# Extra TensorE products of constants placed in five waits of a hybrid backbone kernel

## The reference

```
a    = modulate(rmsnorm(h), shift, scale)
even: y = concat(ssd(...), mlstm(...)) @ w_out     # layer 0, after group norms and gates
odd:  y = concat(window_attention, dense_attention) @ w_out   # layer 1, latent tokens only
h    = h + g1 * y
t    = modulate(rmsnorm(h), sh2, sc2)
route: group = top-1 of softmax(t @ w_group); experts = top-2 of 4 inside the group
moe  = sum over the two experts of gate * (silu(t @ w_gate) * (t @ w_up)) @ w_down
h    = h + g2 * moe
out  = rmsnorm(h_latent)
```

## Time and profile before

| | us |
|---|---|
| median of 3 runs | 1970.26 |
| lowest, highest | 1960.47, 1976.62 |
| the profiled execution, its own time | 1980.49 |
| its span, first to last instruction | 1978.8 |
| mean granted TensorE clock | 0.907 |
| PE busy | 1652.3 (84%) |
| PE weight loads busy | 1006.2 (51%) |
| DVE busy | 848.1 (43%) |
| ACT busy | 520.5 (26%) |
| POOL busy | 273.1 (14%) |

### The profile page before, as it was taken

How to read it: one execution, slowest core, us unless ns; L and a number is a source line. 1 busy time by engine, 2 the same in 40 slices (tenths; PEclk the granted TensorE clock), 3 DMA queues, 4 the chain that set the end, 5 groups by cost and what they waited for, 6 DMA issues and landing times. The chain is left out here.

```text
span 1978.8 us, 17954 instructions
## 1 busy us (share of the span) xinstructions
PE 1652.3 (84%) x6299; PEld 1006.2 (51%) x6299; DVE 848.1 (43%) x1322; ACT 520.5 (26%) x1024; POOL 273.1 (14%) x285
## 2 busy tenths in 40 slices
PE   4999989999959993999939999729969999399960
PEld 2566544444447773455427777514435545277740
DVE  1247448888237773334231111125466634211114
ACT  4122120000055563543011111023246621011111
POOL 0000000000037653121000010011000000010001
PEclk9999989999968886999959999959979999599985
DMA  8345337777187875332047999942030022489963
GB/s 302 117 139 181 121 131 256 277 283 271 58 252 231 228 201 222 141 128 96 22 180 260 349 360 365 350 151 88 8 86 1 1 76 96 184 295 352 347 262 112
DMA packets 153123, 374.90 MB, mean 189 GB/s; under 512 B 14049, under 2 KB 87297, under 8 KB 133089
## 3 DMA queue, kind: packets, MB, share of 16 engines
q1 hardware_dynamic: 128680, 285.45, 42.6%
q0 software_dynamic: 19008, 69.64, 9.2%
q10 hardware_dynamic: 5369, 18.95, 2.3%
HBM read 312.19 MB, written 61.82 MB: 189 GB/s over the span
## 5 line engine op out<-in xcount | busy, mean ns | idle before, releaser
L1821 PE MATMUL ex_ps_gu<-ex_wgu,ex_xT 128*128 128x256 f32 x1152 | 261.4, 386 | 9.5 <-DMA ex_wgu<-in_moe_w_gate_dram 5.7
L629 PE MATMUL ie_pu<-ie_w_zvo,aT_even 128*128 128x512 f32 x576 | 251.7, 598 | 8.4 <-ACTq L736 8.4
L1821 PEld LDWEIGHTS ex_ps_gu<-ex_wgu,ex_xT 128*128 128x128 f32 x1152 | 220.4, 193 | 61.0 <-DMA ex_wgu<-in_moe_w_gate_dram 17.0
L583 PE MATMUL ie_pu<-aT_even,ie_w_conv 128*128 128x512 f32 (+1 forms) x640 | 207.4, 486 | 0.0
L629 PEld LDWEIGHTS ie_pu<-ie_w_zvo,aT_even 128*128 128x128 f32 x576 | 109.6, 192 | 147.7 <-issue 147.7
L1490 PE MATMUL po_ps_y<-po_w,po_yT 128*128 128x512 f32 x384 | 171.0, 605 | 4.2 <-ACT po_w L1368 2.2
L583 PEld LDWEIGHTS ie_pu<-aT_even,ie_w_conv 128*128 128x128 f32 x640 | 121.2, 190 | 84.6 <-issue 76.5
L1839 PE MATMUL ex_ps_d<-ex_wd,ex_hT 128*128 128x512 f32 x288 | 131.2, 598 | 3.4 <-DVE ex_hT L1924 2.1
L1490 PEld LDWEIGHTS po_ps_y<-po_w,po_yT 128*128 128x128 f32 x384 | 73.8, 195 | 93.9 <-issue 89.9
L1920 DVE TENSOR_TENSOR ex_hid<-ex_hid,ex_ps_gu 128x256 f32<-128x256 f32 x36 | 15.2, 421 | 242.4 <-PE ex_ps_gu L1821 242.4
L762 DVE SCALAR_TENSOR_TENSOR ie_y<-ie_pu,pcol,ie_y 128x255 f32<-128x255 f32 x80 | 47.5, 614 | 107.8 <-ACT ie_y L713 106.2
(11 more groups left out here) (429 smaller groups left out, 2360.8 us busy)
## 6 DMA issues: line engine op xcount, KB each, us to landing
ex_wgu<-in_moe_w_gate_dram SPq DMA_DIRECT2D x36, 1024.0 KB, 10.3
ex_wgu<-in_moe_w_up_dram SPq DMA_DIRECT2D x36, 1024.0 KB, 12.1
ex_wd<-in_moe_w_down_dram SPq DMA_DIRECT2D x36, 1024.0 KB, 8.9
ie_w_conv<-in_ada_w_dram SPq DMA_DIRECT2D x27, 1024.0 KB, 5.4
y<-ex_y ACTq DMA_DIRECT2D x36, 512.0 KB, 9.5
ie_y<-in_ada_w_dram SPq DMA_DIRECT2D x13, 1024.0 KB, 5.2
ie_w_zvo<-in_ev_w_in_dram SPq DMA_DIRECT2D x6, 2048.0 KB, 8.6
rc_mt<-ac_rows SPq DMA_DIRECT2D x12, 1024.0 KB, 6.0
```

Source lines behind the costliest of these rows:

```text
L583: last = nc.tensor.matmul(pu[t][:, a:b], w_conv[h][:, k, t * P:(t + 1) * P], aT[:, k, a:b], start=(k == 0), stop=(k == KD - 1))
L629: last = nc.tensor.matmul(pu[bank // 2][:, bank % 2 * BANK:(bank % 2 + 1) * BANK], aT[:, k, T * P:(T + 1) * P], w_zvo[b % 2][:, k, :], sta ...
L1821: last = nc.tensor.matmul(ps_gu[s][part][:, 0:FF], xT[s][:, k, :], wgu[s][:, part, k, :], start=(k == 0), stop=(k == KD - 1))
```

## The change

A helper issues `count` matmuls of two constant 128x128 tiles (the identity and the all-ones tile) into the first 128 columns of a PSUM bank that nobody reads at that point; the next real product there starts anew. Its results are not used. It is called in five places, all on PE's queue, two of them with a new wait ahead of them.

```
+def spare_products(nc, bank, consts, count):
+    for _ in range(count):
+        nc.tensor.matmul(bank[:, 0:P], consts[:, C_ID:C_ID + P], consts[:, C_ONE:C_ONE + P], start=True, stop=True)
...  # phase_out, layer 0 only
             if even:
+                pe.wait_ge(gates_ready, 1)
+                spare_products(nc, ps_r, consts, 24)
                 turn(0)
...  # phase_out, both layers, after the loop over tiles
+            pe.wait_ge(gated, 2 * count)
+            spare_products(nc, ps_y, consts, 14)
             logits(count - 2)
             pe.wait_ge(tT_ready, count - 1)
+            spare_products(nc, ps_y, consts, 8)
             turn_t(count - 1)
             logits(count - 1)
...  # phase_experts, both layers
+            spare_products(nc, ps_d, consts, 30)
             turn_x(0, 0, 1)
...  # phase_in_odd
+            pe.wait_ge(first_scaled, 1)
+            spare_products(nc, ps_w[QD], consts, 30)
             turn_x(0)
```

## The result

The kernel after the change takes 1983.24 us (median of 20 runs, 1971.19 to 1992.03), the kernel before 1971.76 in the same comparison (20 runs, 1960.47 to 1981.85). The ratio is 1.0058, 95% interval 1.0038 to 1.0078: 0.58%, which is 11.4 us, slower (between 7.5 and 15.4). Forecast were 1959.9 and a gain of 10.4.

A forecast was written before the change was run, and what follows sets the result against it. PE, busy 84%, was taken as the bound, idling and then working at half clock at five places. Gains 0.3 + 1.5 + 2.3 + 3.0 + 3.3 + 0 = 10.4 us from the median 1970.26 gave 1959.9, range 1955 to 1964.

The forecast's parts named there:

- C: First expert rows, both layers: 60 spare records fit the wait, transposes and `gate_up` run warm; gains 3.0 and 3.3 us.
- Rival 3: Weights bound the experts, so the expert-stage gain returns as longer waits in the loop; gain 4.1 us, 1966.2; chance 0.12.
- Rival 1: Spare products never raise the clock, so they only delay: 9.4 us slower, 1979.7; chance 0.10.
- A: First output tile, layer 0: spares end 1.4 us late, then transposes run warm; gain 0.3 us (-0.6 to +1.0).
- B: Last logits, both layers: spares make the last `turn_t` and logits warm; gains 1.5 and 2.3 us.
- Rival 4: The logits' 20-column products let the clock fall, so B brings nothing; 6.0 us gained, 1964.3; chance 0.08.
- D: First odd tile: spares delay nothing on the path, first product stays at half clock; gain 0 (-0.3 to +0.2).
- rival 5: In following stretches the clock falls at other places than before; up to 5 us better, 1955; chance 0.08.
- rival 2: The clock falls again behind transposes, at first output tile and last logits; 8.1 us gained, 1962.2; chance 0.12.

The follow-up runs named there:

- all fitted: Kernel before without GpSimd's route-block drain, plus spares: 36 ending route stage, 24 and 8 first output tile, 14 and 4 last logits, 22 odd tile; 1955.01 us.
- the longer spares: As all fitted, but 40 (layer 0) and 46 (layer 1) spares in the route stage and 30 in the odd tile; 1957.75 us, ratio 0.9933.
- all but the experts: The changed kernel without the spare products of the expert stages; 1970.40 us, ratio 1.0006 against the kernel before.
- no drain: The kernel before with the route block closed without GpSimd's drain, no spares anywhere; 1963.14 us, ratio 0.9966.
- 50 ahead of the end: The kernel before with 50 spare products at the end of PE's part of the route block, drain kept; 1971.85 us, ratio 1.0001.

## Why the prediction was wrong

**The step that failed** stands under C: "The block starts when SP has issued its last load, at 1022.2 ... with a start some 0.4 later (an estimate, the barrier shows in no row) PE has 9.6 us until 1032.25". The block starts at 1032.0, and PE has 0.3 us. SP's last load was the last work that I could see, and I took it for the last work there was. The barrier did show in a row, that of SP's wait at the end of the block, and the 15.39 of the earlier trace rows gave the hint: a wait that ends by "DVEq", by a queue and not by a tile, while the transposes read `ex_xg`, which a DMA writes. With the drain gone the same wait ends by "DMA ex_xg". C was to bring 6.3. By the listing it cost 10.9: spares of 8.8 and 9.2 on the path, less 3.2 and 3.4 won back (and 0.5 by waits that were shorter in that profile). The sign named for it, `turn_x` starting after 1034, was just missed at 1033.88, as the whole stage came 6.7 us earlier in that profile; after the listing it started 8.3 later than before.

**Prices of C held.** 60 records were put at 9.7 (9.1 to 10.8) and took 8.94, a little under that range, and 9.35, with the clock rising 4 to 5 us into them. They came cheaper since warm ones start 0.112 us apart; the 0.13 was read up to the start of the next line's product. The transposes came at 1.04 and `gate_up` at 7.14. What failed is the cover alone. Without the drain PE has some 5.2 us (11.8 less the 6.6 until it enters) and 30 products break even, 8.2 against 7.8 without them; behind the listing, where the whole wait is cover, 36 bring 11.8. Rival 3 (the weights) isn't seen: the loop's waits for them are 3.8 and 2.6 us in the change, before 3.5 and 2.2, and the two columns of the table agree, so what `gate_up` gains or loses reaches the end. Rival 1 had a loss in the same place but by another mechanism, and its condition, a clock that doesn't rise, is refuted by 1.04 and 7.14. That its 9.4 lies near the 11.4 is luck.

**A** was to bring 0.3, the profile shows 1.2. The 48 records took 7.48 where 8.1 was expected, the first transposes came 0.6 later against the Silu and the big product 1.2 earlier. That product took 29.16 after 29.17, though the granted clock was 1.00 from its start, where before it rose only at 794: its length isn't set by the clock at its start, as forecast. So the size of A was off, mostly by the price of the spares.

**B** was to bring 1.5 + 2.3, the profile shows 0.8 + 0.4. The 28 records fit (3.39 in 3.87 of idle). The eight products ahead of the last `turn_t` were priced right in layer 0 (`turn_t` 1.1 later, 1.2 forecast), but the last logits took 2.59, not 1.86 (the granted clock was 0.50 from 992), and in layer 1 the 16 records took 3.45, not 2.1 (0.50 from 1678). With four products both layers of all fitted bring what was forecast and more, 2.4 and 3.2. Rival 4, logits that let the clock fall, is half right: in layer 1 the 16 records behind them are slow, but behind the same logits four products keep both layers of all fitted warm, and one of the two in the longer spares. Its price of 6.0 gained counts B's delays of 0.3 + 0.3; with nothing at all from B it would be 6.6.

**D** was put at 0. The first odd product is cold (10.15 behind 8.02 idle, before 9.39 behind 7.41), and all but the experts, with D in it, shows no gain. The product starts 17.3 us after ACT's first scaling in both kernels, so D's spares delay nothing. It ends 0.7 later in the change, but the profiles of kernels without these spares spread from 25.8 to 27.4 after the scaling, before 26.7 and after 27.4. That holds, then. Further on, the third tile's product ran partly cold in the change and its end came 2.3 later than before, but so it did (2.0 and 2.2) with no drain and with 50 ahead of the end, which have no spares in this stage: such falls of the clock move from profile to profile (rival 5), and the gain that rival allowed for isn't seen.

**Transposes and the clock** (rival 2). In the kernel after, 8 transposes and 0.83 us idle stand between the spares and `gate_up`, which is warm at 7.14. By the Trainium skill (TensorE: Matmul & The Clock Gate, Part 4: PE-mode transpose) the full clock doesn't engage for transposes; these runs show that a clock that is up can stay up through eight of them, and run them at its speed (1.04 in place of 1.94), and don't show whether they would raise it. In the first output tile of the change it stayed at 1.00 through sixteen and 2.24 us idle, so A's part of this rival didn't come; its part on the last logits did in layer 0 (0.7 lost), though in all fitted the same transposes and 1.10 idle were followed by 1.96.

**My chances.** "Slower by over 1%" had 0.03 and didn't come (0.58%), but the time fell outside the range, on the side that I had given 0.10. What the range lacked was the case that the entry is set by the gathers.

## What to carry to other kernels

Ahead of filling a wait with work, ask which of two waits it is: for data, inside the block, or for the block itself. Read the waits of every queue at the end of the block before, and take a wait that ends by a queue's name for a barrier until shown otherwise. In this kernel filler paid ahead of the barrier, where it ended close to the real work, and shortening the barrier itself was worth 0.34% with no filler at all. PE can do without the drain here because it waits on the gathers' own semaphores.

## What the runs showed of the hardware

**GpSimd's drain waits for its indirect gathers.** It lasted 13.26 and 13.89 us, and held PE and SP at the end of the block. In the six kernels that keep it, twelve blocks in all, it lasted 12.95 to 15.82 us and closed 0.11 to 0.13 us after the second gather's last rows each time. Without it PE waited for the first gather alone and entered its work 4.4 us earlier after the listing (11.8 in place of 16.2).

**Gaps behind warm spares.** Each is followed by eight transposes, 0.83 us idle and the first `gate_up`. Gap, and what `gate_up` took: 0.45, 0.58, 1.08 and 2.16 us were followed by 7.14 or 7.15; 2.41, 2.86, 2.96 and 3.32 by 10.20, 9.89, 9.60 and 10.05. Between them it isn't clean: 1.33 and 2.38 were followed by 8.83 and 8.58, a clock that fell midway. The output stage of the change went both ways too: behind sixteen transposes and 2.24 us idle the granted clock was 1.00, behind sixteen and 2.01 at the next tile it fell to 0.50. What tells 1.33 from 2.16 stays open.

**The gap can't be fixed by a count.** The same 62 products left 0.45 us in one layer and 2.16 in the other. The wait's end hangs on a DMA: 16.3 and 18.7 us after the listing here, 16.2 and 16.8 in the kernel before.
